# Expert rows summed in DRAM by accumulating scatters, in place of a combination at the end of a decoder layer

## What is computed

```python
def hier_moe(h, ...):                      # h = rms_norm(x, norm2_g)
    grp = jnp.argmax(g_logits, axis=-1)    # one of 4 groups
    top_val, top_idx = lax.top_k(e_in, 2)  # two of its 8 experts
    w_top = jax.nn.softmax(top_val, axis=-1) * p_grp[:, None]
    ...
    ys = (silu(xb @ w_gate[e]) * (xb @ w_up[e])) @ w_down[e]     # per block of rows xb of expert e
    ys = ys * w_flat[order][:, None]
    out = jnp.zeros((m, D_MODEL)).at[t_s].add(ys)                # each row gets two terms

x = x + mix @ w_o                          # the residual rows, x2 in the kernel
x = x + hier_moe(rms_norm(x, norm2_g), ...)
y = rms_norm(x, norm_f_g)                  # f_out in the kernel
```

## Time and profile before

| | us |
|---|---|
| median of 3 runs | 1766.57 |
| profiled execution | 1764.86 |
| its span | 1763.3 |
| PE busy | 1647.6 (93%) |
| DVE busy | 1043.2 (59%) |
| ACT busy | 833.8 (47%) |
| POOL busy | 137.8 (8%) |
| DMA, mean over the span | 172 GB/s |

### The profile page before, as it was taken

One profiled execution on the slowest core, in us unless ns is written; L12 is line 12 of the kernel. 1 busy time (PEld: TensorE's weight loads), 2 busy tenths in 40 slices (PEclk: granted clock), 3 DMA queues, 4 the chain that ended last, 5 costly groups with the idle time before them and its releaser, 6 DMA issues.

```text
span 1763.3 us, 26050 instructions
## 1 busy us (share of the span) xinstructions
PE 1647.6 (93%) x9491; PEld 1470.7 (83%) x9491; DVE 1043.2 (59%) x1780; ACT 833.8 (47%) x1210; POOL 137.8 (8%) x163
## 2 busy tenths in 40 slices
PE   5999999999999999999999998599999999999960
PEld 4899899999998999999999886488888888888850
DVE  5322466666655331114224465698989989898947
ACT  5000355555555331113112222487777787877833
POOL 1100000000000100000000012111010111111000
PEclk9999999999999999999999999799999999999985
DMA  5242111111111311122113413699999999999807
GB/s 160 79 120 84 40 49 37 48 48 36 36 47 37 101 37 48 48 107 85 48 48 130 159 73 126 247 374 385 380 376 377 372 384 384 382 383 368 344 26 288
DMA packets 130548, 304.16 MB, mean 172 GB/s; under 512 B 29364, under 2 KB 91032, under 8 KB 105632
## 3 DMA queue, kind: packets, MB, share of 16 engines
q1 hardware_dynamic: 115344, 267.27, 41.7%
q0 software_dynamic: 15152, 36.18, 5.6%
HBM read 286.97 MB, written 35.19 MB: 183 GB/s over the span
## 4 chain that ended last, share of the span: by engine, by line
PE 92%; DVE 4%; DMA 1%; ACT 1%; issue 1%; POOLq 1%; SPq 0%; POOL 0%; ACTq 0%; DVEq 0%
PE bank L998 10%; PE bank L669 9%; PE bank L671 9%; PE bank L670 9%; PE bank L986 7%; PE bank L988 7%; PE bank L987 7%; PE bank L814 6%; PE bank L815 5%; PE bank L816 5%; PE bank L763 2%; PE bank L944 2%; PE bank L946 2%; PE bank L948 2%; PE bank L977 2%; PE bank L773 2%
## 5 line engine op out<-in xcount | busy, mean ns | idle before, releaser
L1804 DVE TENSOR_TENSOR e_lo<-e_raw,e_hi 128x2048 fp32r<-128x2048 f32 x192 | 434.0, 2287 | 60.4 <-ACT e_hi L1296 58.9
L1296 ACT ACTIVATE e_hi<-e_raw 128x2048 fp32r<-128x2048 f32 x192 | 365.5, 1922 | 59.3 <-PE bank L988 37.1
L986 PE MATMUL bank<-e_hi,xT_hi 128*128 128x512 f32 x512 | 206.5, 403 | 5.0 <-DVE xT_lo L1809 5.0
L1080 ACT ACTIVATE w_hi<-w_raw 128x1024 fp32r<-128x1024 f32 x68 | 71.6, 1053 | 284.5 <-PE bank L671 252.7
L669 PE MATMUL bank<-h_hi,w_hi 128*128 128x344 f32 x624 | 202.7, 325 | 1.1 <-DVE h_lo L1414 1.1
L988 PE MATMUL bank<-e_hi,xT_lo 128*128 128x512 f32 x512 | 202.8, 396 | 0.0
L987 PE MATMUL bank<-e_lo,xT_hi 128*128 128x512 f32 x512 | 202.2, 395 | 0.0
L670 PE MATMUL bank<-h_lo,w_hi 128*128 128x344 f32 x624 | 199.8, 320 | 0.0
L671 PE MATMUL bank<-h_hi,w_lo 128*128 128x344 f32 x624 | 199.8, 320 | 0.0
L814 PE MATMUL bank<-h_hi,w_hi 128*128 128x344 f32 x576 | 196.6, 341 | 2.0 <-DVE w_lo L1395 2.0
L815 PE MATMUL bank<-h_lo,w_hi 128*128 128x344 f32 x576 | 184.0, 320 | 0.0
(11 more groups left out here) (314 smaller groups left out, 3035.6 us busy)
## 6 DMA issues: line engine op xcount, KB each, us to landing
e_raw<-in_w_e_gate_dram SPq DMA_DIRECT2D x64, 1024.0 KB, 7.4
e_raw<-in_w_e_up_dram SPq DMA_DIRECT2D x64, 1024.0 KB, 7.1
e_raw<-in_w_e_down_dram SPq DMA_DIRECT2D x64, 1024.0 KB, 7.1
w_raw<-in_w_in_dram SPq DMA_DIRECT2D x104, 256.0 KB, 3.1
f_y<-expert_rows SPq DMA_DIRECT2D x16, 512.0 KB, 9.9
a_spill<-y_sb POOLq DMA_DIRECT2D x8, 516.0 KB, 2.9
a_raw<-a_spill SPq DMA_DIRECT2D x2, 2064.0 KB, 9.7
x_tok<-in_x_prompt_dram SPq DMA_DIRECT2D x4, 1024.0 KB, 10.9
```

The costliest lines, as they stand in the source:

```text
L986: pe.matmul(out, xT_hi[:, par, kk, :], wh, start=kk == 0, stop=False)
L1296: A.activation(e_hi[:, slot % 4, :], e_raw[slot][:, :], ACT.Copy).then_inc(e_hi_done, 1)
L1804: V.tensor_tensor(e_lo[slot][:, :], e_raw[slot][:, :], e_hi[:, slot % 4, :].bitcast(F32), ALU.subtract).then_inc(e_lo_done, 1)
```

## The change

The sum over a row's two experts and the residual moves from the end of the kernel into DRAM:

- A DRAM tensor `summed_rows` (1032 x 1024) takes the place of `expert_rows`. SP writes the residual rows x2 into it, tile by tile (`begin_sums`).
- The scatters add to it (`compute_op=ALU.add`), with `gidx` as rows. Each waits on GpSimd for the one before it.
- The rows must be weighted before they are scattered, so each expert needs the weights in the order of its list. `weight_lists` in DRAM is built like `token_lists`: blanked near the start, filled by 18 indirect writes (`enter_weights`), read back as `wl` (128 x 32). ScalarE applies them as the scale of its copy into `y_out`.
- The end loads one row set straight into `f_out` (9 DMAs); `combine` is gone. A first Sqrt on a single column stands before ScalarE's last loop.
- GpSimd loads the overflow count before the last two scatters, and sends `rows_written` by a plain increment in place of the drain.

```diff
+            def begin_sums(n, rows):
+                sp.wait_ge(x2_done, n + 1)
+                sp.dma_start(sum_dram[bass.ds(n * P, rows), :], x2[0:rows, bass.ds(n, 1), :].rearrange("p a d -> p (a d)")).then_inc(sums_begun, 16)
...
             with sp.Fori(1, 4) as i:
                 for b in range(2):
                     load_x(i * 2 + b, b, False)
+                    begin_sums(i * 2 + (b - 2), P)
             sp.wait_ge(sq2_done, 7)
             sp.dma_start(x_in[0:B8, 0, :], x_sample[:, 0, :]).then_inc(x_again[0], 16)
+            begin_sums(6, P)
 
             sp.wait_ge(proj_done, NT)
             for s in range(4, 12):
                 if s == 9:
 
+                    begin_sums(7, P)
+                    begin_sums(8, B8)
...
-                for k in range(2):
-                    sp.dma_start(f_y[k][0:rows, n, :], y_dram[n * P + k * T:n * P + k * T + rows, :]).then_inc(f_loaded[n], 16)
+                sp.dma_start(f_out[0:rows, n, :], sum_dram[n * P:n * P + rows, :]).then_inc(f_loaded[n], 16)
...
+            pool.dma_start(wl_dram.rearrange("(p q) o -> p (q o)", p=P), list_init[:, :].bitcast(F32)).then_inc(list_blank, 16)
...
             def scatter_rows(e):
                 pool.wait_ge(y_stored, e + 1)
-                pool.indirect_dma_start(out=y_dram, out_offset=bass.IndirectOffsetOnAxis(ap=lst[:, e:e + 1], axis=0),
-                                        in_=y_out[:, :], in_offset=None, bounds_check=2 * T - 1, oob_is_err=False).then_inc(scattered, 16)
+                if e > 0:
+                    pool.wait_ge(scattered, 16 * e)
+                pool.indirect_dma_start(out=sum_dram, out_offset=bass.IndirectOffsetOnAxis(ap=gidx[:, e:e + 1], axis=0),
+                                        in_=y_out[:, :], in_offset=None, bounds_check=T - 1, oob_is_err=False,
+                                        compute_op=ALU.add).then_inc(scattered, 16)
+
+            def enter_weights(n, rows):
+
+                for k in range(2):
+                    pool.indirect_dma_start(out=wl_dram, out_offset=bass.IndirectOffsetOnAxis(ap=adr[0:rows, 2 * n + k:2 * n + k + 1], axis=0),
+                                            in_=wts[0:rows, n, k:k + 1], in_offset=None,
+                                            bounds_check=LISTROWS * NE - 1, oob_is_err=False).then_inc(weighed, 16)
 
             for e in range(2):
                 gather_rows(e)
+            pool.wait_ge(wts_done, 1)
+            for n in range(NT):
+                enter_weights(n, P if n < 8 else B8)
             for e in range(NE):
                 if e + 2 < NE:
                     pool.wait_ge(xT_psum, e + 1)
                     gather_rows(e + 2)
+                if e == 0:
+                    pool.wait_ge(weighed, WEIGHED_FROM + 32 * NT)
+                    pool.dma_start(wl[:, :], wl_dram[0:P * NE, :].rearrange("(r e) o -> r (e o)", e=NE)).then_inc(wl_loaded, 16)
+                    pool.wait_ge(sums_begun, SUMS_FROM + 16 * NT)
                 if e >= 2:
                     scatter_rows(e - 2)
+            pool.wait_ge(ov_sbuf, 3)
+            n_ov = pool.value_load(ov_t[0:1, 2 * OVF:2 * OVF + 1], min_val=0, max_val=OVF)
             for e in range(NE - 2, NE):
                 scatter_rows(e)
             pool.wait_ge(scattered, 16 * NE)
-
-
-            pool.wait_ge(ov_sbuf, 3)
             pool.sem_inc(v_free, 1)
-            n_ov = pool.value_load(ov_t[0:1, 2 * OVF:2 * OVF + 1], min_val=0, max_val=OVF)
...
-            pool.drain().then_inc(rows_written, 1)
+            pool.sem_inc(rows_written, 1)
...
+                else:
+                    act.wait_ge(wl_loaded, WL_FROM + 16)
                 for x in range(2):
-                    ins = A.activation(y_out[:, 512 * x:512 * x + 512], bank[2 + x][:, :], ACT.Copy)
+                    ins = A.activation(y_out[:, 512 * x:512 * x + 512], bank[2 + x][:, :], ACT.Copy, scale=wl[:, e:e + 1] if isinstance(e, int) else wl[:, bass.ds(e, 1)])
...
-            act.wait_ge(rows_written, 1)
+            A.activation(warm[:, :], eps[:, :], ACT.Sqrt)
             for n in range(NT):
                 rows = P if n < 8 else B8
-                act.wait_ge(f_sum, n + 1)
+                act.wait_ge(f_loaded[n], F_FROM + 16)
...
-            def combine(n):
-                r = rows_of(n)
-                dve.wait_ge(f_loaded[n], F_FROM + 32)
-                out = f_out[0:r, n, :]
-                final.after(V.scalar_tensor_tensor(out, f_y[0][0:r, n, :], wts[0:r, n, 0:1], x2[0:r, n, :], ALU.mult, ALU.add))
-                V.scalar_tensor_tensor(out, f_y[1][0:r, n, :], wts[0:r, n, 1:2], out, ALU.mult, ALU.add).then_inc(f_sum, 1)
...
-            for n in range(NT + 1):
-                if n < NT:
-                    combine(n)
-                if n > 0:
-                    finish(n - 1)
+            for n in range(NT):
+                finish(n)
```

More of the change, by code:

```diff
@@ L111, in program @@
     xn_dram = nc.dram_tensor("normed_rows", (T, D), F32).ap()
-    y_dram = nc.dram_tensor("expert_rows", (2 * T, D), F32).ap()
+    sum_dram = nc.dram_tensor("summed_rows", (T, D), F32).ap()
+    wl_dram = nc.dram_tensor("weight_lists", (LISTROWS * NE, 1), F32).ap()
     list_dram = nc.dram_tensor("token_lists", (LISTROWS * NE, 1), U32).ap()
@@ L261, in program @@
         scol = small("scol", [1], U32)
+        wl = small("wl", [NE])
+        wcol = small("wcol", [1])
+        warm = small("warm", [1])
         e_raw = [at(f"e_raw{i}", RING + 8192 * i if i < 4 else 8192 * (i - 4), [2048]) for i in range(12)]
@@ L279, in program @@
         v_aT = at("v_aT", R3 + 4096, [4, P])
-        f_y = [at(f"f_y{k}", 36864 * k, [NT, D]) for k in range(2)]
         f_out = at("f_out", R5, [NT, D])
@@ L340, in program @@
             sem("v_gu"), sem("v_silu"), sem("v_act"), sem("v_apsum"), sem("v_aT_done"), sem("v_ypsum"), sem("v_y"), sem("v_scattered"))
-        rows_written, gf_loaded, f_sum, f_sq, f_root, f_done, f_stored = (
-            sem("rows_written"), sem("gf_loaded"), sem("f_sum"), sem("f_sq"), sem("f_root"), sem("f_done"),
-            sem("f_stored"))
+        rows_written, gf_loaded, f_sq, f_root, f_done, f_stored = (
+            sem("rows_written"), sem("gf_loaded"), sem("f_sq"), sem("f_root"), sem("f_done"), sem("f_stored"))
+        wts_done = sem("wts_done")
+        sums_begun, SUMS_FROM = x_loaded[0], 16
+        weighed, WEIGHED_FROM = cols_loaded, 32
+        wl_loaded, WL_FROM = consts_loaded, 16 * 4
         f_loaded, F_FROM = e_loaded[0:NT], 16 * 16
@@ L575, in _ @@
             pool.dma_start(rb[:, NG:NG + NE], b_router_expert[0].partition_broadcast(P)).then_inc(router_loaded, 16)
-            pool.wait_ge(list_blank, 16)
+            pool.wait_ge(list_blank, 32)
             def write_xn(n, rows):
@@ L644, in _ @@
                         pool.dma_start(scol[:, 0:1], list_dram[bass.ds(bk * (P * NE), P * NE), :].rearrange("(r e) o -> r (e o)", e=NE)[:, bass.ds(ex, 1)],
+                                       allow_slow_non_contiguous=True).then_inc(v_col, 16)
+                        pool.dma_start(wcol[:, 0:1], wl_dram[bass.ds(bk * (P * NE), P * NE), :].rearrange("(r e) o -> r (e o)", e=NE)[:, bass.ds(ex, 1)],
                                        allow_slow_non_contiguous=True).then_inc(v_col, 16)
@@ L652, in _ @@
                         carry(1).then_inc(idled, 1)
-                        pool.indirect_dma_start(out=y_dram, out_offset=bass.IndirectOffsetOnAxis(ap=scol[:, 0:1], axis=0),
-                                                in_=y_out[:, :], in_offset=None, bounds_check=2 * T - 1, oob_is_err=False).then_inc(v_scattered, 16)
+                        pool.indirect_dma_start(out=sum_dram, out_offset=bass.IndirectOffsetOnAxis(ap=gcol[:, 0:1], axis=0),
+                                                in_=y_out[:, :], in_offset=None, bounds_check=T - 1, oob_is_err=False,
+                                                compute_op=ALU.add).then_inc(v_scattered, 16)
                         pool.wait_ge(idled, i * 2 + 2)
@@ L1373, in _ @@
                         act.wait_ge(v_free, i + 1)
+                        act.wait_ge(v_idx, i + 1)
                         for x in range(2):
-                            ins = A.activation(y_out[:, 512 * x:512 * x + 512], bank[2 + x][:, :], ACT.Copy)
+                            ins = A.activation(y_out[:, 512 * x:512 * x + 512], bank[2 + x][:, :], ACT.Copy, scale=wcol[:, 0:1])
                         ins.then_inc(v_y, 1)
-            act.wait_ge(rows_written, 1)
+            A.activation(warm[:, :], eps[:, :], ACT.Sqrt)
             for n in range(NT):
                 rows = P if n < 8 else B8
-                act.wait_ge(f_sum, n + 1)
+                act.wait_ge(f_loaded[n], F_FROM + 16)
                 A.activation(f_junk[0:rows, :], f_out[0:rows, n, :], ACT.Square, accum_out=ssq[0:rows, n:n + 1]).then_inc(f_sq, 1)
@@ L1798, in _ @@
             step.after(V.reciprocal(wts[:, :, 0], wsum[:, :]))
```

(4 more changed lines are left out.)

## The result

The changed kernel takes 1754.22 us, the median of 4 runs (1753.14 to 1755.43), against 1766.14 before in the same session; the ratio is 0.9934, with a 95% interval of 0.9917 to 0.9952. So 11.9 us are won where 27 were forecast. The measured time lies in the wide range of the forecast (1734 to 1756), but above the range of its likeliest case (1734 to 1745). The profiled span is 1753.8 for the 1736.1 forecast: 17.7 us are missing. The signs are as foretold, the sizes are not, and the place of most of the loss is one that the forecast had called covered.

A forecast was written before the change was run, and what follows sets the result against it. VectorE was taken to bound the serial last 56 us, TensorE what precedes. Tail -28.4, residual writes +0.5, blanking +0.3, experts +0.4 sum to -27.2: 1739.4 us by the median; likeliest case 1734 to 1745, 8 in 10 1734 to 1756.

The forecast's parts named there:

- The start of the expert stage: GpSimd's 18 weight writes run to 1139, gather 2 lands at 1144 to 1148, before TensorE wants it at 1151: covered.
- Rival D: Gather 2 late: weight writes at half speed in the DMA's backlog, landing 5 us after 1151; 1744, counted within the forecast's 0.72.
- Each expert: In the expert stage, adding scatters land in 9.5 us and cause no wait; +0.4 us for all of it.
- Rival A: Expert stage: adding overloads the half of the DMA engines carrying all rows; 1746 (0.07), or 1785 if tripled (0.09 with C).
- Rival C: Each expert waits for the scatter's landing, from 16.1 us on; 1796 at 18 us; chance 0.09 together with A tripled.
- Step 2: Tail: the last scatter, now adding in DRAM, lands 1.2 us later than 3.18, with bounds of 0 and +3.2.
- Step 8: Tail: DMA, not VectorE, sets the end; 8.45 MB at 413 GB/s take 20.5 us, ending at 1734.9, later by 2.4.
- Step 4: Tail: GpSimd's drain of 8.41 us goes; SyncE's first load comes at 1712.0, not 1719.7.
- rival B: Tail: the drain's 8.4 us stay because the semaphore increment waits too; 1747.8, chance 0.09.
- Steps 1, 3, 5 and 6: Tail: scaled y_out write +0.1; count load ahead, 0.5 stays; first load of nine 4.2; first tile 2.9 us.
- step 7: Tail: eight more tiles at VectorE's pace of 1.40 us each, 11.2 us, then 2.2 for the last store.
- The start of the program: Before the expert stage: SP's residual-row writes +0.5 us and blanking the weight list +0.3.

The follow-up runs named there:

- experiment 7: Changed kernel plus a stage after its last store, timing GpSimd weight writes beside VectorE work and single plain or adding scatters; its total time is not compared.
- Experiment 2: Changed kernel without the 18 weight writes and weight list; weights go to DRAM by token and are gathered for each expert: 1743.96 us.
- experiment 3: Changed kernel with plain scatters that add nothing, so the sums are left out: 1748.36 us.
- experiment 4: Changed kernel with lists loaded so that each expert's real rows lie on both halves of the partitions: 1748.59 us.
- experiment 8: Changed kernel with the last eight large stores at half width (columns 0 to 511 alone): 1751.62 us.
- experiment 1: Changed kernel with gather 2 issued ahead of sixteen of the 18 weight writes: 1750.34 us.
- experiment 6: Changed kernel with GpSimd's drain put back: 1762.05 us; and the kernel before with a plain semaphore increment for its drain: 1757.73 us.

## Why the prediction came out as it did

The 17.7 us between the forecast span and the measured one, by its own steps:

- **The start of the expert stage, 9.65 us: the step that failed.** "Such a write takes 0.99 us and 0.30 to the next": the price was right for the rows it was read from, L586 in the residual stage. The 18 new ones stand beside the e_lo splits, and there half of them take twice to three times as long. That put gather 2 at 1150.5 instead of 1139, TensorE's wait at 7.63 us, and some slow clock behind it (granted 0.93 from 1150 to 1200). Rival D named the place, but gave 5 us and another cause, the DMA's backlog; experiment 7 has the same slow writes with no backlog at all. Experiment 2 gives the whole back.
- **Each expert, 3.4 us.** The forecast took 399 GB/s against 426 and +0.4. The mean over 16 engines was the wrong measure. Rival A had the right one: weights 6.29 MB an expert in 17.96 us are 82% of 426, and q0 on half of the engines is twice 7.8%, together 98% before, which leaves 0.4 us an expert. An adding row takes its engine 0.17 us longer (328 for 159 ns), so 8 rows take 1.35 more; less the 0.4, that is an estimate of 0.95 us of debt an expert. Rival A had 0.77 with a doubled scatter, and measured are 0.8. The growth of landing then took up 17 us, as rival A said, and 3.8 came through for its 7. Experiments 3 and 4 show both halves of that mechanism. The forecast had given it a chance of 0.07. Rival C fell: a scatter lands in 10.2 us (9.5 forecast, 16.1 allowed).
- **Step 2, 1.3 us.** Adding costs the last scatter 2.55 us, not 1.2: inside its bounds of 0 and 3.2, and nearer to "the whole landing doubles". The reason given there was wrong: 0.65 us for the data assumes all 16 engines. The 53 rows of this scatter lie on 8; at 159 ns that is 1.05 us plain, at 328 ns 2.2 adding. GpSimd's issue is 0.55 us longer, and the rest are the slow first rows (0.5 to 0.9 us in this scatter).
- **Step 8, 2.6 us.** The mechanism was right (experiment 8), the rate was too high: the packets of the trace run from 1729.3 to 1752.9, so 8.45 MB took 23.6 us, 358 GB/s and not 413. The first came 1.0 us after SyncE's first load instead of 0.4, and the last ended 0.9 us before the end instead of 2. Loads and stores ran at 354 to 368 from 1730 to 1740, and at 400 to 419 later, mostly with stores alone.
- **Step 4, the drain:** right, 7.8 and 8.1 us for 8.41; rival B fell. Steps 1, 3, 5 and 6 held within 0.6 us each, and the table load of ScalarE runs at 1721, before the sums land. In step 7 the pace was right, 1.40 us from pass to pass, but the eight tiles took 12.4 us for 11.2, as VectorE stood idle twice (0.65 and 0.48 us) behind late loads; this was hidden, since the DMA set the end.
- **The start of the program, +1.3 for +0.8: agreement by luck.** The first gather is issued at 1114.66 (before: 1113.34), but in experiments 1, 3 and 6 (the drain put back), with the same instructions up to there, it came at 1115.39, 1115.15 and 1112.87; and in the kernel before without its drain, GpSimd's clearing of xg came at 1100.73 for 1098.82, with nothing changed ahead of it. The shift is made in one place: against the kernel before, ScalarE is 0.3 us early at 188 us and 1.3 late at 221, and stays so to 1100. The windows of TensorE at 192 us, of the changed kernel and of experiment 2, show the clock there:

```profile
192.00:194.00 2.00, 2.00 (x9) 0.50 0.76 225
```

```profile
192.00:194.00 2.00, 2.00 (x14) 1.00 0.81 240
```

In the one TensorE is granted 1.2 GHz and does 9 matmuls, in the other 2.4 and 14. The kernel before had 1.00 there too, and so had the changed kernel with its drain put back, whose first gather came 0.5 us earlier than that of before. So the 0.8 us forecast for the duplicated blanking and the writes of residual rows shows nowhere. Why the clock falls at 192 us in some executions is not shown.

The terms are 9.65 + 3.4 + 1.3 + 2.6 + 0.5, 17.5 of 17.7. What stays open is the rate of 354 to 368 GB/s while loads and stores mix, why the first rows of an adding scatter are slow, and what the drain waits for.

## What to carry to other kernels

Price an instruction by rows that have the same neighbours, not only the same form: an indirect write added to GpSimd's queue took double while VectorE worked on two operands in SBUF, and what is queued behind it pays. Count a DMA by what its busiest engine carries, and let a row that is added be twice a plain one there; lists that are half empty belong on both halves of the partitions. And when an early step is moved out of the way, look at its second reader, for the wait goes there.

## What the runs showed of the hardware

- A GpSimd indirect write of one element a partition takes 0.97 us to issue with VectorE idle or reading one operand from PSUM (128x512), 2.02 beside a subtraction of two SBUF tiles (128x2048), and 2.23 beside an SBUF copy (128x2048).
- A scatter that adds: 1.55 us to issue for 1.00, landing 6.4 us for 3.3 (64 rows on partitions 0 to 63) and 4.6 for 2.7 (on both halves), alone; 10.2 for 8.0 beside the weights. A row of 4 KB takes its engine 328 ns for 159; alone, the first rows take 0.5 to 1.2 us.
- A drain of GpSimd behind the landing of its last scatter took 8.3 to 8.4 us.
